# Four further products of the all-ones matrix behind the statistic of three post-norms

## The reference

```python
h = rms_norm(x, norm_mix_pre[l]);  y = hybrid_mixer(h, ...)
x = x + rms_norm(y, norm_mix_post[l])
h = rms_norm(x, norm_mem_pre[l]);  y = memory_cross_attention(h, ...)
x = x + rms_norm(y, norm_mem_post[l])
h = rms_norm(x, norm_mlp_pre[l]);  y = squared_relu_mlp(h, w_up[l], w_down[l])
x = x + rms_norm(y, norm_mlp_post[l])
```

## Time and profile before

| | |
|---|---|
| median of three runs | 1816.08 us (1813.85 to 1817.47) |
| the profiled execution, own time | 1815.37 us |
| its span, first to last instruction | 1813.6 us |
| mean granted TensorE clock, share of full speed | 0.994 |
| TensorE matmul busy | 1773.4 us (98%) |
| VectorE, ScalarE, GpSimd busy | 1029.9, 463.9, 1074.8 us |

### The profile page before, as it was taken

One profiled execution on the slowest core, in us unless ns is written; L12 is line 12 of the kernel. 1 busy time (PEld: TensorE's weight loads), 2 busy tenths in 40 slices (PEclk: granted clock), 3 DMA queues, 4 the chain that ended last, 5 costly groups with the idle time before them and its releaser, 6 DMA issues.

```text
span 1813.6 us, 22611 instructions
## 1 busy us (share of the span) xinstructions
PE 1773.4 (98%) x8364; PEld 1435.2 (79%) x8364; DVE 1029.9 (57%) x1194; ACT 463.9 (26%) x931; POOL 1074.8 (59%) x604
## 2 busy tenths in 40 slices
PE   9998999999999999999999999999999999999997
PEld 7775777788888877767888888887887888888886
DVE  5999355835252675175625262696766562616177
ACT  6427335401010222163201010212335320202011
POOL 7594452566666665434666666665344566666672
PEclk9999999999999999999999999999999999999999
DMA  6232221233333333211333333332222223333331
GB/s 241 70 100 64 70 82 47 79 96 93 102 95 93 98 100 93 82 47 59 93 98 99 93 94 103 93 93 82 70 70 59 82 93 99 98 93 95 102 93 47
DMA packets 46591, 161.44 MB, mean 89 GB/s; under 512 B 5232, under 2 KB 7792, under 8 KB 46384
## 3 DMA queue, kind: packets, MB, share of 16 engines
q1 hardware_dynamic: 45088, 157.31, 28.5%
q10 hardware_dynamic: 1424, 3.02, 0.5%
HBM read 158.21 MB, written 2.10 MB: 88 GB/s over the span
## 4 chain that ended last, share of the span: by engine, by line
PE 92%; DVE 4%; ACT 2%; issue 1%; POOL 1%; DMA 0%; SPq 0%; DVEq 0%; POOLq 0%; ACTq 0%
PE bank L406 21%; PE bank L407 21%; PE bank L408 21%; PE bank L454 3%; PE bank L455 3%; PE bank L456 3%; PE bank L474 1%; PE bank L476 1%; PE bank L475 1%; PE bank L1002 1%; PE bank L1038 1%; PE bank L1004 1%; PE bank L1003 1%; DVE bank L1773 1%; PE bank L1053 1%
## 5 line engine op out<-in xcount | busy, mean ns | idle before, releaser
L320 POOL TENSOR_TENSOR WL<-RAW,WH 128x1024 fp32r<-128x1024 f32 x291 | 740.8, 2546 | 24.3
L315 POOL TENSOR_SCALAR WH<-RAW 128x1024 fp32r<-128x1024 f32 x291 | 313.2, 1076 | 670.4 <-PE bank L408 363.0
L406 PE MATMUL bank<-AH,WH 128*128 128x512 f32 x848 | 332.6, 392 | 0.0
L408 PE MATMUL bank<-AH,WL 128*128 128x512 f32 x848 | 330.0, 389 | 0.0
L407 PE MATMUL bank<-AL,WH 128*128 128x512 f32 x848 | 330.0, 389 | 0.0
L406 PE MATMUL bank<-HH,WH 128*128 128x512 f32 x832 | 325.2, 391 | 0.0
L407 PE MATMUL bank<-HL,WH 128*128 128x512 f32 x832 | 324.0, 389 | 0.0
L408 PE MATMUL bank<-HH,WL 128*128 128x512 f32 x832 | 323.7, 389 | 0.0
L1428 ACT ACTIVATE TMP<-bank 128x512 f32<-128x512 f32 x96 | 57.3, 596 | 776.9 <-PE bank L408 739.1
L2049 DVE TENSOR_TENSOR HL<-TMP,HH 128x512 fp32r<-128x512 f32 x96 | 239.0, 2490 | 4.0 <-ACT HH L1433 0.7
L2055 DVE TENSOR_TENSOR Y<-Y,bank 128x512 f32<-128x512 f32 x72 | 49.5, 688 | 309.3 <-PE bank L408 309.3
(11 more groups left out here) (390 smaller groups left out, 2355.4 us busy)
## 6 DMA issues: line engine op xcount, KB each, us to landing
RAW<-wstream SPq DMA_DIRECT2D x291, 512.0 KB, 3.5
out<-Y SPq DMA_DIRECT2D x8, 256.0 KB, 2.2
X<-xT SPq DMA_DIRECT2D x3, 512.0 KB, 8.1
TMP<-memT ACTq DMA_DIRECT2D x1, 1024.0 KB, 7.2
MIX<-bands ACTq DMA_DIRECT2D x1, 768.0 KB, 4.6
RAW<-wstream SPq DMA_DIRECT2D x2, 256.0 KB, 3.7
X<-xT SPq DMA_DIRECT2D x2, 256.0 KB, 4.0
BF<-masks ACTq DMA_DIRECT2D x1, 352.0 KB, 4.0
```

The source lines that it names most:

```text
L315: nc.gpsimd.tensor_scalar(WH[:, s, :, :].rearrange("p k n -> p (k n)"), RAW[:, s, :], 1.0, 1.0, ALU.mult, ALU.mult).then_inc(sem("w_high"), 1)
L320: nc.gpsimd.tensor_tensor(WL[:, s, :, :].rearrange("p k n -> p (k n)"), RAW[:, s, :], f32(WH[:, s, :, :].rearrange("p k n -> p (k n)")), A ...
L406: mm(bank, WH[:, slot, k, :], h(k), start=(k == 0), stop=False)
L408: last = mm(bank, WL[:, slot, k, :], h(k), start=False, stop=(k == KT - 1))
```

## The change

Behind the second product of `post_stat`, TensorE waits for the eighth `yg` (ScalarE has read the last tile of y out of PSUM) and then multiplies the all-ones matrix by the tile of squares of y that it just used, four times, into a bank that is free at that time: bank 3 for `o1`, bank 0 for `o2` and `m3`. Nobody reads the results; the next quad starts those banks afresh. Nothing else in the program changes; the lines behind the first hunk are two higher than before.

```diff
 OPENING = 10
+BRIDGE = {"o1": 3, "o2": 0, "m3": 0}
+BRIDGE_PRODUCTS = 4
 MK_READ = (2, 6)
...
                 mm(B[7][:], ONES[:], SUM, start=True, stop=False)
                 pe.wait_ge(sem(f"{p}_ysq"), nth(f"{p}_ysq", 8))
                 mm(B[7][:], ONES[:], TMP[:, 5, :], start=False, stop=True).then_inc(sem(f"{p}_ystat"), 1)
+                pe.wait_ge(sem(f"{p}_yg"), nth(f"{p}_yg", 8))
+                for _ in range(BRIDGE_PRODUCTS):
+                    mm(B[BRIDGE[p]][:], ONES[:], TMP[:, 5, :], start=True, stop=True)
```

## The result

| | before | after |
|---|---|---|
| median of six runs each | 1815.75 us (1813.85 to 1817.47) | 1821.74 us (1820.58 to 1823.78) |
| ratio, 95% interval | | 1.0035 [1.0022, 1.0048] |
| profiled execution, own time and span | 1815.37, 1813.6 us | 1821.23, 1819.4 us |
| mean granted TensorE clock | 0.994 | 0.998 |

The kernel is 6.0 us slower, with a higher clock. Medians leave out two far slower executions of e2 (2978 and 4588 us) and one of the kernel before (2222 us).

A forecast was written before the change was run, and what follows sets the result against it. TensorE was taken to bound the kernel, with work queued for 98% of the span. The profiled 1815.37 us plus 6.1 us lost in the three quads gave 1821.5 us, range 1813.0 to 1823.0.

The forecast's parts named there:

- The added products fill idle time: Behind each post-norm's second statistic product, four products take 3.44 us in TensorE's idle wait for AH tile 0, costing nothing.
- What full speed gives at first: In the three quads at full clock, k = 7 starts about 19.3 us after the first product, 5.4 us gained.
- P: Start of a quad's first product, from which the forecast counts times within that quad.
- E: End of AL tile 1 in a quad, put at P + 2.77.
- A dead heat of AL tiles 3 and 5 with POOL's second pass: In each quad, AL tiles 3 and 5 start with POOL's second pass; if POOL wins both, 6.1 us lost.
- POOL wins: At equal recorded starts POOL takes the shared port first by 0.07 us, in both heats; chance 0.58.
- VectorE winning both heats: Rival: in the quads AL gets the port first both times, TensorE never waits; -5.4 us, 1810.0; chance 0.18.
- Split heats: Rival: VectorE wins one heat in a quad, POOL the other; +0.4 us; chance 0.21, quads that differ included.
- The waits: New waits of TensorE for AL of about 1.8 us, two in each quad, some 10 us in all.

The follow-up runs named there:

- e2: The changed kernel with four products, but the quads' slots of k = 1, 3 and 5 handed back to POOL three products later; 1812.23 us.
- e1: Five added products per post-norm instead of the changed kernel's four; 1811.48 us, 0.9977 of the kernel before.
- e7: Five added products instead of the changed kernel's four, and POOL's second pass in two halves; 1804.19 us, 0.9937 of the kernel before.
- e4: Two added products per post-norm instead of the changed kernel's four; 1821.45 us, 1.0036 of the kernel before.
- e6: The kernel before, without added products, with POOL's second pass in two halves; 1809.23 us, 0.9963 of the kernel before.

## Why the prediction was right

The forecast was 1821.5 us and slower; measured were 1821.74.

- **The added products fill idle time: right**, with one slip. Their passes come 0.43 us apart, so 0.86 us for a product as forecast, and full clock held. But `yg` does hold them up a little: the first weight load behind it waits 0.28 us for ScalarE's last tile of y, and the products start 0.96 us behind the second statistic product, not 0.86. The idle time left was 0.30 us instead of 0.5, so the slip cost nothing.
- **What full speed gives at first: right.** k = 1 at P + 2.85 and k = 2 at P + 5.70; forecast E + 0.05 = P + 2.82 and E + 2.93 = P + 5.70. If nothing else were in the way, k = 7 would come at about P + 19.3: e1 reaches P + 19.5, the late start of k = 1 included, and gains 3.9 us by its median.
- **A dead heat of AL tiles 3 and 5 with POOL's second pass: right.** Six heats, with starts 0.00 to 0.02 us apart. From k = 3 to k = 7 the forecast was P + 10.18, 13.06, 17.54, 20.42, 23.14; `mq` has 10.16, 13.02, 17.47, 20.35, 23.07. The loss was put at 6.1 us and is 5.96 in the quads.
- **POOL wins: right, in line with the reason given.** The telling case is the second heat of the quad behind `o2`, where AL is recorded first and loses:

```profile
342.01 2.94 DVE L1667 SCALAR_TENSOR_TENSOR AL<-X,VC,AH 128x512 fp32r<-128x512 f32 x1
342.03 2.37 POOL L322 TENSOR_TENSOR WL<-RAW,WH 128x1024 fp32r<-128x1024 f32 x1
```

  Ahead by 0.02 us AL lost, ahead by 0.07 or 0.08 it won (e7). So POOL's advantage lies between 0.02 and 0.07 us, and the 0.07 that I worked out is at or just above the upper end; that AL would need a lead of over about 0.1 to be safe was too much. The instant inside an instruction at which it is decided is not in any trace; that there is one is inferred. The Trainium skill (SBUF — State Buffer, section on the two separate sides) says that whoever starts first holds the port for the whole instruction; the traces agree with the whole instruction, but the recorded start is not the instant that decides.
- **The rivals.** VectorE winning both heats is what e1 is, and it has about the forecast size (quads 58.5 us, forecast 57.9). That it did not come about here is a matter of less than 0.1 us: the starts were worked out to 0.03 us beside an advantage of that order, so there was luck in the outcome, and my chance of 0.58 was no more than the heat allowed. Split heats did not occur: both come from one event with the same distances, and went the same way in all three quads. I had put them at 0.21, as if they were more independent.
- **The waits** of 1.8 us each appear as 1.6 in the list. Counted from tile starts the stall is as forecast: k = 3 begins 4.46 us behind k = 2 instead of 2.72, 1.74 more. The list counts from the recorded end of the last product, 0.39 us behind its start, while in a steady stream the next starts after 0.23.

## What to carry to other kernels

An edit that makes one engine earlier also makes its hand-backs earlier: here the full clock brought the return of a weight slot forward by 1.4 to 2.5 us, onto AL tile 3, which it had not met before, so replay the other engines against it, above all two that share a resource for a whole instruction. Long instructions on such a resource are worth splitting: the length of the winner's instruction is the price of a lost heat, and half passes gained more here (6.3 us alone) than the full clock did in e1 (3.9 us). A small sweep (here 3, 4, 5, 6 products) is a cheap test for such a coincidence: a cost of the products themselves would have grown with their number, and the heat showed as a step.

## What was not expected of the hardware

- The granted clock may fall while TensorE is already back at work: in e4's profile it was full at 248.92, when the products began again after 2.02 us idle, and fell between 248.9 and 250.8 (mean 0.90), to be at half until past 253.2. The same is in the rows of the kernel before: behind `o2` the quad starts at 325.87, and the stretch from 326.15 is the one at half.
- Five executions out of six with the same two products differ from the sixth by 6.4 to 9.1 us; nothing in the program differs.
- Halving POOL's pass costs it 100 us of busy time (740.8 us for 291 whole passes before, 839.5 for 582 halves in e6) and the kernel is 6.3 us faster. POOL is busy for 59% of the span before.
